# The delta rule's triangular inverse: its doublings and their turns from 128- and 64-wide products to 32x32 products on the block diagonal

## The reference, cut to what matters

```
tri = jnp.where(strict, jnp.einsum('bhnld,bhnmd->bhnlm', kb, kc) * decay, 0.0) + jnp.eye(L, dtype=f32)
u = lax.linalg.triangular_solve(tri, vb, left_side=True, lower=True)
w = lax.linalg.triangular_solve(tri, kb * jnp.exp(gc)[..., None], left_side=True, lower=True)
qk = jnp.einsum('bhnld,bhnmd->bhnlm', qc, kc) * decay

def step(state, inp):
    uu, ww, qkk, qd, kd, dec = inp
    v_new = uu - jnp.einsum('bhld,bhdv->bhlv', ww, state)
    o = jnp.einsum('bhld,bhdv->bhlv', qd, state) + jnp.einsum('bhlm,bhmv->bhlv', qkk, v_new)
    state = state * dec[..., None, None] + jnp.einsum('bhld,bhlv->bhdv', kd, v_new)
    return state, o
```

## Time and profile before

| | us |
|---|---|
| median of 3 runs | 1409.67 (1409.17 to 1409.72) |
| the profiled execution, its own time | 1406.89 |
| its span | 1405.2 |
| outside the span | 1.69 |
| GDN: from the first turn of the inverse to the first output product | 1198.06 to 1234.75 |

### The profile page before, as it was taken

How to read it: one execution, slowest core, us unless ns; L and a number is a source line. 1 busy time by engine, 2 the same in 40 slices (tenths; PEclk the granted TensorE clock), 3 DMA queues, 4 the chain that set the end, 5 groups by cost and what they waited for, 6 DMA issues and landing times. The chain is left out here.

```text
span 1405.2 us, 19630 instructions
## 1 busy us (share of the span) xinstructions
PE 1320.7 (94%) x7848; PEld 1074.9 (76%) x7848; DVE 906.8 (65%) x1255; ACT 672.0 (48%) x968; POOL 218.3 (16%) x123
## 2 busy tenths in 40 slices
PE   6998889999999989899999989989999989989998
PEld 2784558678888786677888868978887878868987
DVE  1687895778778667668665474655455587554664
ACT  2544343264443355555443345655563767436561
POOL 0001551131000040304000001200001342500300
PEclk9999998999999989999999999999999999999999
DMA  8861560539889664367675449715543531038840
GB/s 313 308 205 49 179 242 2 194 128 319 282 298 310 219 193 169 132 202 232 225 241 182 148 117 207 223 50 158 186 143 107 184 133 61 32 101 169 213 148 30
DMA packets 160635, 247.24 MB, mean 176 GB/s; under 512 B 15064, under 2 KB 100028, under 8 KB 160032
## 3 DMA queue, kind: packets, MB, share of 16 engines
q1 hardware_dynamic: 159216, 239.61, 53.7%
q0 software_dynamic: 1328, 6.38, 1.2%
HBM read 244.86 MB, written 4.24 MB: 177 GB/s over the span
## 5 line engine op out<-in xcount | busy, mean ns | idle before, releaser
L199 DVE TENSOR_TENSOR w_lo<-w_raw,w_hi 128x2048 fp32r<-128x2048 f32 (+3 forms) x176 | 402.6, 2295 | 240.0 <-ACT w_hi L190 239.9
L217 PE MATMUL ps<-w_hi,act_hi 128*128 128x512 f32 (+4 forms) x1216 | 472.6, 389 | 16.1 <-DVE act_lo L877 6.4
L219 PE MATMUL ps<-w_hi,act_lo 128*128 128x512 f32 (+4 forms) x1216 | 462.8, 381 | 0.0
L218 PE MATMUL ps<-w_lo,act_hi 128*128 128x512 f32 (+4 forms) x1216 | 462.5, 380 | 0.0
L190 ACT CAST w_hi<-w_raw 128x2048 fp32r<-128x2048 f32 (+3 forms) x176 | 316.8, 1806 | 248.3 <-PE ps L219 206.9
L217 PEld LDWEIGHTS ps<-w_hi,act_hi 128*128 128x128 f32 x1216 | 230.8, 190 | 62.3 <-issue 15.6
L219 PEld LDWEIGHTS ps<-w_hi,act_lo 128*128 128x128 f32 x1216 | 230.3, 189 | 37.2
L218 PEld LDWEIGHTS ps<-w_lo,act_hi 128*128 128x128 f32 x1216 | 230.8, 190 | 34.4 <-issue 1.0
L684 POOL TENSOR_TENSOR nstat<-nstat,con 128x1 f32<-128x1 f32 x8 | 5.4, 680 | 416.9 <-DVE nstat L679 416.9
L217 PE MATMUL ps<-w_hi,ffn_gh 128*128 128x512 f32 x176 | 69.7, 396 | 0.0
L219 PE MATMUL ps<-w_hi,ffn_gl 128*128 128x512 f32 x176 | 68.6, 390 | 0.0
(11 more groups left out here) (516 smaller groups left out, 1734.2 us busy)
## 6 DMA issues: line engine op xcount, KB each, us to landing
w_raw<-in_ffn_w_in SPq DMA_DIRECT2D x88, 512.0 KB, 4.8
w_raw<-in_fox_w_in SPq DMA_DIRECT2D x32, 912.0 KB, 8.3
w_raw<-in_ada_w SPq DMA_DIRECT2D x28, 1024.0 KB, 5.9
w_raw<-in_ffn_w_out SPq DMA_DIRECT2D x20, 1024.0 KB, 5.4
w_raw<-in_rwkv_w_rkv SPq DMA_DIRECT2D x12, 1024.0 KB, 7.0
con<-in_ada_w SPq DMA_DIRECT2D x48, 256.0 KB, 5.2
w_raw<-in_gla_w_in SPq DMA_DIRECT2D x10, 896.0 KB, 4.7
w_raw<-in_gdn_w_in SPq DMA_DIRECT2D x10, 896.0 KB, 4.9
```

What stands on the lines that cost most here:

```text
L199: self.nc.vector.tensor_tensor(lo[:, s, 0:c["nk"], 0:c["width"]], self.raw[:, c["slot"], 0:c["nk"], 0:c["width"]], hi[:, s, 0:c["nk"], 0:c ...
L217: nc.tensor.matmul(out(t)[:, 0:w], xh[:, k, tok], hi[:, s, j, 0:w], start=start, stop=False)
L218: nc.tensor.matmul(out(t)[:, 0:w], xh[:, k, tok], lo[:, s, j, 0:w], start=False, stop=False)
L219: return nc.tensor.matmul(out(t)[:, 0:w], xl[:, k, tok], hi[:, s, j, 0:w], start=False, stop=stop)
```

## The change

It changes how the products of levels 4 to 6 and their turns are cut, and nothing outside the GDN mixer.

- The turn of level 4 (`turn4`) and of level 5 (`turn5`) is no longer 8 transposes of 128x128 for each q but products of 32x32 blocks of `up` with the identity: 32 for each q at level 4, each with 16 moving columns, and 24 at level 5, with 32.
- `ax4` and `xax4` are 32 products for each q: one for each head and 32-row block, at row group and column group c for block c, with 16 moving columns. `ax5` is 16 products of 32x32 and `xax5` 24. `ax6` and `xax6` stay 8 products of 64x64 each, but neighbouring heads go to opposite halves of the PSUM partitions.
- The order of the groups on PE is changed at level 4: both turns come first.
- ACT copies less in each of `low4_out`, `x4`, `x5` and `low_out`, but `low_out` and `x6` are two copies each. At level 5 DVE copies `low` first and then `up`; level 6 is two copies for each q.
- POOL blanks a corner of `low` at the stage's start.
- The splits of weights and the Silu activations keep their places.

```
+        def blocks(q, out, lhs, right, done, rows=range(4)):
+            for h in range(VH):
+                for c in rows:
+                    s = slice(32 * c, 32 * c + 32)
+                    r = nc.tensor.matmul(out(h, s), lhs(VH * q + h, s), right(VH * q + h, s), start=True, stop=True)
+            r.then_inc(sem("g_" + done), 1)
+
+        def sides(q, bank, lhs, right, done):
+            for h in range(VH):
+                side = slice(64 * (h % 2), 64 * (h % 2) + 64)
+                r = nc.tensor.matmul(ps[side, bank, 64 * h:64 * h + 64], lhs(VH * q + h), right(VH * q + h), start=True, stop=True)
+            r.then_inc(sem("g_" + done), 1)
...
+        def turn4(q):
+            blocks(q, lambda h, s: ps[s, q, 16 * h:16 * h + 16], lambda th, s: up[s, th, s], lambda th, s: core.c("ident")[s, left(s)], "turn4")
 
         def ax4(q):
-            each_half(q, lambda h: ps[:, 2 + 2 * q, 64 * h:64 * h + 64].rearrange("p (m s) -> p m s", s=16), lambda th, h: am[:, th, :],
-                      lambda th, h: up[:, th, :].rearrange("p (m two s) -> p m two s", two=2, s=16)[:, :, 1, :], "ax4")
+            blocks(q, lambda h, s: ps[s, 2 + 2 * q, 16 * h:16 * h + 16], lambda th, s: am[s, th, s], lambda th, s: up[s, th, right(s)], "ax4")
...
+        def turn5(q):
+            pe.wait_ge(sem("g_up4"), 4 * q + 4)
+            blocks(q, lambda h, s: ps[s, q, 32 * h:32 * h + 32], lambda th, s: up[s, th, s], lambda th, s: core.c("ident")[s, s], "turn5", range(3))
 
         def ax5(q):
-            pe.wait_ge(sem("g_up4"), 4 * q + 4)
-            each_half(q, lambda h: split(2 + 2 * q, h), lambda th, h: am[:, th, :], lambda th, h: odd(up[:, th, :]), "ax5")
+            for h in range(VH):
+                for b in (0, 64):
+                    even, odd = slice(b, b + 32), slice(b + 32, b + 64)
+                    r = nc.tensor.matmul(ps[even, 2 + 2 * q, 32 * h:32 * h + 32], am[odd, VH * q + h, even], up[odd, VH * q + h, odd], start=True, stop=True)
+            r.then_inc(sem("g_ax5"), 1)
...
         def x4(q):
             act.wait_ge(sem("g_ax4"), q + 1)
-            copy(mm.x[q][:, :, :], heads8(2 + 2 * q)).then_inc(sem("g_x4"), 1)
+            copy(mm.x[q][:, :, 0:16], heads16(2 + 2 * q)).then_inc(sem("g_x4"), 1)
...
         def level6(q):
             dve.wait_ge(sem("g_up6_mm"), q + 1)
-            v.tensor_copy(up[0:64, VH * q:VH * q + VH, 64:P], heads8(2 + 2 * q)[0:64, :, :]).then_inc(sem("g_up6"), 1)
+            for i in range(2):
+                v.tensor_copy(up[0:64, VH * q + i:VH * q + VH:2, 64:P], heads8(2 + 2 * q)[64 * i:64 * i + 64, i:VH:2, :]).then_inc(sem("g_up6"), 1)
```

More of the change, by code:

```diff
@@ L3620, in pe @@
         tok = lambda t: slice(t * P, t * P + P)
-        odd = lambda ap: ap.rearrange("p (c two s) -> p c two s", two=2, s=32)[:, :, 1, :]
         def turn(s, t, bank):
@@ L3653, in value_conv @@
             r.then_inc(sem("g_conv"), 1)
[L3655 to L3666, removed]
@@ L3695, in xax5 @@
         def xax5(q):
             pe.wait_ge(sem("g_x5"), q + 1)
-            pe.wait_ge(sem("g_low"), q + 1)
+            pe.wait_ge(sem("g_low"), 2 * q + 1)
             x = mm.x[q]
-            each(q, lambda h: ps[0:96, 3 + 2 * q, 64 * h:64 * h + 64], lambda th, h: low[:, th, :], lambda th, h: x[:, h, :], "up5_mm")
-            each(q, lambda h: ps[0:32, 2 + 2 * q, 32 * h:32 * h + 32], lambda th, h: x[:, h, 0:32], lambda th, h: low[:, th, 0:32], "low5_mm")
+            for h in range(VH):
+                th, cols = VH * q + h, slice(32 * h, 32 * h + 32)
+                r = nc.tensor.matmul(ps[32:64, 3 + 2 * q, cols], x[0:32, h, 0:32], low[0:32, th, 0:32], start=True, stop=True)
+                if h == VH - 1:
+                    r.then_inc(sem("g_low5_mm"), 1)
+                for b in (0, 64):
+                    even = slice(b, b + 32)
+                    r = nc.tensor.matmul(ps[even, 2 + 2 * q, cols], low[even, th, 0:32], x[even, h, 0:32], start=True, stop=True)
@@ L3702, in ax6 @@
+            r.then_inc(sem("g_up5_mm"), 1)
         def ax6(q):
+            pe.wait_ge(sem("g_low5"), q + 1)
             pe.wait_ge(sem("g_up5"), 2 * q + 2)
-            each(q, lambda h: ps[0:64, 3 + 2 * q, 64 * h:64 * h + 64], lambda th, h: am[64:P, th, 0:64], lambda th, h: up[64:P, th, 64:P], "ax6")
+            sides(q, 3 + 2 * q, lambda th: am[64:P, th, 0:64], lambda th: up[64:P, th, 64:P], "ax6")
         def xax6(q):
-            pe.wait_ge(sem("g_x6"), q + 1)
-            pe.wait_ge(sem("g_low5"), q + 1)
@@ L3709, in xax6 @@
-            x = mm.x[q]
-            each(q, lambda h: ps[0:64, 2 + 2 * q, 64 * h:64 * h + 64], lambda th, h: low[0:64, th, 0:64], lambda th, h: x[0:64, h, :], "up6_mm")
+            pe.wait_ge(sem("g_x6"), 2 * q + 2)
+            pe.wait_ge(sem("g_low"), 2 * q + 2)
+            pe.wait_ge(sem("g_low_blank"), 1)
+            sides(q, 2 + 2 * q, lambda th: low[0:64, th, 0:64], lambda th: mm.x[q][0:64, th - VH * q, :], "up6_mm")
         def new_values(t, bank):
-            pe.wait_ge(sem("g_up6"), t + 1)
+            pe.wait_ge(sem("g_up6"), 2 * t + 2)
@@ L3768, in pe @@
         pe.wait_ge(sem("g_up_back"), 4)
-        turn_up(0, 0)
+        turn4(0)
+        turn4(1)
         ax4(0)
         ax4(1)
-        turn_up(1, 0)
         xax4(0)
         xax4(1)
-        turn_up(0, 1)
+        turn5(0)
         ax5(0)
-        turn_up(1, 1)
+        turn5(1)
         ax5(1)
@@ L3786, in pe @@
         next_state(0)
-        pe.wait_ge(sem("g_up6"), 2)
+        pe.wait_ge(sem("g_up6"), 4)
         from_state(2, QH, "ks_mm")
@@ L3835, in act, with low4_out @@
             split.act(act, min(b + 1, 3))
+        def low4_out(q):
+            act.wait_ge(sem("g_turn4"), q + 1)
+            copy(mm.low4[:, VH * q:VH * q + VH, 0:16], heads16(q)).then_inc(sem("g_low4"), 1)
         def low_out(q):
[L3838 to L3843, removed]
+            act.wait_ge(sem("g_turn5"), q + 1)
+            th = slice(VH * q, VH * q + VH)
+            copy(low[0:96, th, 0:32], heads32(q)[0:96]).then_inc(sem("g_low"), 1)
+            copy(low[32:64, th, 32:64], heads32(q)[32:64]).then_inc(sem("g_low"), 1)
         def x4(q):
             act.wait_ge(sem("g_ax4"), q + 1)
-            copy(mm.x[q][:, :, :], heads8(2 + 2 * q)).then_inc(sem("g_x4"), 1)
+            copy(mm.x[q][:, :, 0:16], heads16(2 + 2 * q)).then_inc(sem("g_x4"), 1)
         def x5(q):
             act.wait_ge(sem("g_ax5"), q + 1)
-            act.wait_ge(sem("g_up4_mm"), q + 1)
-            copy(mm.x[q][:, :, :], heads8(2 + 2 * q)).then_inc(sem("g_x5"), 1)
+            copy(mm.x[q][:, :, 0:32], heads32(2 + 2 * q)).then_inc(sem("g_x5"), 1)
         def x6(q):
             act.wait_ge(sem("g_ax6"), q + 1)
-            act.wait_ge(sem("g_low5_mm"), q + 1)
-            copy(mm.x[q][0:64, :, :], heads8(3 + 2 * q)[0:64, :, :]).then_inc(sem("g_x6"), 1)
+            act.wait_ge(sem("g_up5_mm"), q + 1)
+            for i in range(2):
+                copy(mm.x[q][0:64, i:VH:2, :], heads8(3 + 2 * q)[64 * i:64 * i + 64, i:VH:2, :]).then_inc(sem("g_x6"), 1)
         def values(t, bank):
@@ L3870, in act @@
         low4_out(0)
+        low4_out(1)
         x4(0)
         x4(1)
-        low4_out(1)
         for t in range(NT):
@@ L3938, in level4 @@
             dve.wait_ge(sem("g_up4_mm"), q + 1)
[L3939 to L3942, removed]
+            for b in range(0, P, 32):
+                v.tensor_copy(up[b:b + 16, VH * q:VH * q + VH, b + 16:b + 32], heads16(3 + 2 * q)[b:b + 16]).then_inc(sem("g_up4"), 1)
         def level5(q):
             th = slice(VH * q, VH * q + VH)
+            dve.wait_ge(sem("g_low5_mm"), q + 1)
+            v.tensor_copy(low[32:64, th, 0:32], heads32(3 + 2 * q)[32:64]).then_inc(sem("g_low5"), 1)
             dve.wait_ge(sem("g_up5_mm"), q + 1)
[L3947 to L3951, removed]
+            for b in (0, 64):
+                v.tensor_copy(up[b:b + 32, th, b + 32:b + 64], heads32(2 + 2 * q)[b:b + 32]).then_inc(sem("g_up5"), 1)
         def level6(q):
             dve.wait_ge(sem("g_up6_mm"), q + 1)
-            v.tensor_copy(up[0:64, VH * q:VH * q + VH, 64:P], heads8(2 + 2 * q)[0:64, :, :]).then_inc(sem("g_up6"), 1)
+            for i in range(2):
+                v.tensor_copy(up[0:64, VH * q + i:VH * q + VH:2, 64:P], heads8(2 + 2 * q)[64 * i:64 * i + 64, i:VH:2, :]).then_inc(sem("g_up6"), 1)
         def root(t):
@@ L4013, in pool @@
         nc.gpsimd.memset(mm.ut[:, :, 0:3], 0.0).then_inc(sem("g_pad"), 1)
+        nc.gpsimd.memset(mm.low[0:32, :, 32:64], 0.0).then_inc(sem("g_low_blank"), 1)
         nc.gpsimd.memset(up[:, 0:NT * VH, :], 0.0).then_inc(sem("g_blank"), 1)
```

20 lines of the change are left out of this document (8 added, 12 removed).

## The result

The changed kernel is slower: a median of 1411.38 us over 20 runs against 1405.72 for 20 runs of the kernel before, a ratio of 1.004 (95% interval 1.0028 to 1.0051). The forecast was 1408.6 from a base of 1409.67, 1.1 us won; measured are some 5.7 lost. Runs of the kernel before spread from 1401 to 1417 us, so the lengths inside the GDN stage say more than totals (level 4 starts 5.20 or 5.21 us after the first turn in all seven profiles whose products up to there are the old ones). The profiled execution took 1415.59.

The account below looks back on a forecast made before the run. PE, busy 94% of the span, was taken as the bound, with DVE soon bounding the second length. Forecast 1.1 + 2.0 - 2.0 = 1.1 us won, 1409.67 to 1408.6 us, range 1405.4 to 1411.6.

Parts of the forecast that it names:

- the small edit that was put at nothing: Whole program: 352 more passes to fetch and issue, priced at 0 because no row showed a wait on that.
- First length: First turn to DVE's first level-4 copy: 4.1 us instead of 5.21 at 12 ns a thin pass, 1.1 us won.
- Second length: Level 4 to new_values, bound by DVE's list: 11.4 us (full clock) or 11.8 (half) instead of 13.83, 2.0 won.
- Clock: Falls to half during the doublings' thin products, stays low into the dense passes after new_values: 2.0 us lost.
- Rivals: Clock holds, 1406.1, chance 0.25; clock low for long, 1410.6, chance 0.15; dear passes, 1412.7, chance 0.17.
- Rival (3): Doublings' thin passes cost 24 ns through a floor or no overlap: 3.0 us lost, 1412.7; chance 0.17.

Follow-up runs that it names:

- e_l56: Kernel before with only the products and copies of levels 5 and 6 in the new form, turns and level 4 old; ratio 1.0002 to before.
- e_aftw: Changed kernel with 20 wide constant products between PE's groups; first turn to first output product 46.77 us against 41.80 in the changed kernel.
- e_late: Changed kernel with the last 1 MB weight load of gdn_out requested only after level 6; first turn to first output product 41.20 us against 41.80.
- e_turns: Changed kernel with the old 128x128 transposes and wide copies back for both turns; first turn to first output product 38.88 us against 41.80.
- e_stack: Changed kernel with turns as one full 128-row product per head against stacked identities; first turn to first output product 44.43 us against 41.80.
- e_pad: Kernel before with 176 extra unused 32x32x16 products, as many added instructions as the change; ratio 1.0028 to before.
- e_warm2: e_l56 plus five short constant products (2.8 us) in PE's waits; first turn to first output product 35.54 us against 36.69 before.

## Why the prediction was wrong, point by point

- **The step that failed** is the small edit that was put at nothing, the fetch of instructions: "The program has 352 more passes to fetch and issue (704 for 352); no row shows a wait on that now, so I put 0". The runs showed four stops of 8.20 us in its place, of which 3.64 came in the first length and 4.56 in the second, each ended by a packet of instructions. The rows before had no such wait because PE used its 256 instructions more slowly than they came: in the earlier trace rows 241 passes in 13.83 us, 35 instructions a us, against 256 per 3.5 us, 73 a us. At 8.6 ns a pass the thin groups ask for some 230 a us, a packet every 1.1 us; in the trace of before no two packets of q8 started less than 3.8 us apart (220.28 and 224.06, in the RWKV stage's thin products). The zero was never set against the new rate.
- **First length.** Forecast 4.1 us, measured 7.08, of which 3.64 are the gap and 3.44 the rest. The pass was 8.6 ns and not 12 at full clock, so the term's own size erred the good way. I had said a fetch limit would show "in the thin pass"; it shows between passes, at every 128th.
- **Second length.** Forecast 11.8 at low clock, measured 14.96 with 4.56 us of gaps, partly beside DVE's split. DVE waited 1.14 us for PE ahead of level 5, where the prediction allowed 0.5. Without gaps e_l56 has 11.85, with DVE busy for 11.12 of it, so the account by DVE's list holds when PE is fed.
- **Clock.** Forecast: a fall between 1201 and 1206, low until some 4 us into the dense passes, 2.0 lost. Measured: a fall at 1203.9, low until 4.7 us after 1223.13, tail 2.11 longer. That term was right, and e_aftw shows its cause on this kernel with constants between its groups: with the clock at 1.00 the tail is 17.55. What made it fall is less sure here, since 1203.9 lies 0.8 us into the first gap, and the gap itself may have had a part. In e_late, e_turns and e_stack the fall lies within the first gap too, while e_pad had a gap of 1.24 and no fall. In e_l56 it fell at 1210.9 without any gap; the longest idle stretch of PE in the doublings before that was 0.67 us. The Trainium skill ("TensorE: Matmul & The Clock Gate", "HAM oscillation — how this bites in real kernels") ties the fall to long idle gaps. The changed kernel could agree with that; e_l56 and the earlier trace rows do not, as the clock fell there with PE mostly busy on small tiles.
- **Rivals.** None named the supply. Rival (3) had the right sign for another reason, a dear pass, against 8.6 ns measured. That its 1412.7 is near 1411.38 is luck: it loses 3.0 us where 5.7 were lost, and the kernel before came out at 1405.72 instead of 1409.67. The same 3.95 us put the measured total inside the stated 1405.4 to 1411.6, though the loss is larger than any rival's. The floor of 25 ns that the Trainium skill states ("TensorE: Matmul & The Clock Gate", "Wait — 56ns, not 53.3ns?") does not hold here as a floor on the pass (8.6 ns measured); that 256 instructions in 3.5 us are 27 ns a pass on average is another matter.
- **Sum.** 5.21 + 13.83 became 22.04: +3.0; tail +2.1; rest +0.6; 5.7, as the medians say. The 8.2 us of gaps are more than the 3.0, because PE's idle time in the doublings grew by 8.6 and its busy time shrank by 5.6. Supply and clock can't be wholly parted in this kernel, as the fall lies within a gap. That the change without gaps and with the clock held would win is shown for levels 5 and 6 only; for level 4, e_turns shows a start 1.25 us earlier, and no run shows the whole change fed in time.

## What to carry to other kernels

Cutting a product into tiles that run side by side makes PE's passes cheap and its instructions many. Divide the instructions of the new stretch by its new length, and compare that with the rate at which a trace shows the engine being fed (here 256 per 3.5 us). Stops with "issue" inside a group of like products, at equal counts of instructions and each just behind a packet of the instruction queue, are the sign to look for. In these kernels small tiles also left PE at its lower clock for the dense work behind them; wide products in the waits kept it up, and they have to be sized to the waits (between first turn and first output product, 2.8 us of them won 1.2 us and 6 us lost 1.6).

## What the runs showed of the hardware that was not expected

- PE was fed in batches of some 256 instructions, one per 3.5 to 4.0 us once it had run dry (after, e_late). In every one of the eleven stops in five kernels it went on 1.3 to 1.5 us after a 16,384-byte packet of the instruction queue had ended, and the next packet started only 1.0 to 1.6 us after that. The first stop was 1.3 us longer where a 1 MB load ran (3.64 against 2.33).
- Four 32x32 tiles at separate row and column groups, writing one PSUM bank at separate partitions, ran at 8.6 ns a pass at full clock; in e_aftw three ran at 11 and two at 15.9, with 32 moving columns instead of 16.
- A pass with 128 columns of weights and only 16 moving columns took 112 ns at full clock (e_stack).
- The low clock after the first output product (3.4 us long before; 6.8 after the change, from 1.4 us ahead of that product) went when PE's wait ahead of it was filled.
- 2.8 us of wide products spread over the second length kept the clock at 1.00 there (e_warm2), where it had fallen without them (e_l56).
